# A macaron encoder layer on one core: seven-product blocks in the first up projection, and attention scores in three rounded passes

## The reference, cut to what matters

```
c_act = silu(c)
mod = (c_act @ w_ada + b_ada).reshape(B, 3, 3, D)        # shift, scale, gate of each sub-layer
h = x * (1 + scale) + shift
g, u = split(h @ ffn1_w_in, 2);  y = (silu(g) * u) @ ffn1_w_out            # 1024 -> 2 x 2816 -> 1024
x = layernorm(ALPHA * x + 0.5 * gate * y)
proj = h @ w_in;  cq, ckv, k_rope_raw, u = split(proj)
s = (q_nope . k_nope + q_rope . k_rope) * sm_scale       # 8 heads, 64 + 32 wide, chunk-causal
out = softmax(where(mask, s, -inf)) @ v
y = concat([out, pooled(u)]) @ w_out
... a second FFN like the first
```

## Time and profile before

| | |
|---|---|
| time, median of 3 runs (lowest, highest) | 938.01 us (937.66, 938.11) |
| the profiled execution's own time | 938.53 us |
| its span, from first to last instruction | 936.7 us |
| PE busy, share of the span | 924.4 us, 99% |
| DVE, ACT, POOL busy | 600.4, 422.3, 276.1 us |
| TensorE clock granted, mean | 0.998 |

### The profile page before, as it was taken

One profiled execution on the slowest core, in us unless ns is written; L12 is line 12 of the kernel. 1 busy time (PEld: TensorE's weight loads), 2 busy tenths in 40 slices (PEclk: granted clock), 3 DMA queues, 4 the chain that ended last, 5 costly groups with the idle time before them and its releaser, 6 DMA issues.

```text
span 936.7 us, 12697 instructions
## 1 busy us (share of the span) xinstructions
PE 924.4 (99%) x4845; PEld 777.8 (83%) x4845; DVE 600.4 (64%) x875; ACT 422.3 (45%) x673; POOL 276.1 (29%) x239
## 2 busy tenths in 40 slices
PE   8999999999999999999999999999999999999997
PEld 5788888888888888787776677889999999888886
DVE  6956776545454964687775577787777877533334
ACT  6753223332322132483576646655556555322124
POOL 0021111111113522155863655832111110035124
PEclk9999999999999999999999999999999999999999
DMA  9936556556553663314411112286777775623302
GB/s 356 379 117 211 189 192 199 193 180 206 192 175 129 200 240 116 102 68 135 118 63 46 45 54 82 70 255 158 183 190 180 179 193 147 225 79 107 124 18 90
DMA packets 50507, 144.88 MB, mean 155 GB/s; under 512 B 5264, under 2 KB 7440, under 8 KB 50448
## 3 DMA queue, kind: packets, MB, share of 16 engines
q1 hardware_dynamic: 45008, 134.65, 42.3%
q0 software_dynamic: 4896, 8.92, 6.0%
q10 hardware_dynamic: 544, 0.52, 0.2%
HBM read 138.83 MB, written 4.19 MB: 153 GB/s over the span
## 4 chain that ended last, share of the span: by engine, by line
PE 94%; DVE 2%; DMA 2%; ACT 1%; issue 1%; SPq 1%; ACTq 0%; DVEq 0%
PE bank L890 23%; PE bank L892 23%; PE bank L891 23%; PE bank L1001 6%; PE bank L1003 6%; PE bank L1002 6%; PE bank L1307 2%; PE bank L1331 1%; DMA ada_first<-ada_w 1%; PE bank L1318 1%; DMA raw_d<-wunits 1%; PE bank L975 1%; PE bank L1071 1%; PE bank L976 1%; PE bank L969 1%
## 5 line engine op out<-in xcount | busy, mean ns | idle before, releaser
L1434 DVE TENSOR_TENSOR w_lo<-raw,w_hi 128x1024 fp32r<-128x1024 f32 (+1 forms) x117 | 160.7, 1383 | 132.2 <-ACT w_hi L1406 131.8
L890 PE MATMUL bank<-h_hi,w_hi 128*128 128x512 f32 x455 | 178.7, 393 | 0.0
L892 PE MATMUL bank<-h_hi,w_lo 128*128 128x512 f32 x455 | 177.2, 389 | 0.0
L891 PE MATMUL bank<-h_lo,w_hi 128*128 128x512 f32 x455 | 177.2, 389 | 0.0
L1406 ACT ACTIVATE w_hi<-raw 128x1024 fp32r<-128x1024 f32 (+1 forms) x118 | 118.7, 1023 | 117.5 <-PE bank L892 111.5
L890 PE MATMUL bank<-a_hi,w_hi 128*128 128x512 f32 (+1 forms) x338 | 128.0, 379 | 0.0
L891 PE MATMUL bank<-a_lo,w_hi 128*128 128x512 f32 (+1 forms) x338 | 127.7, 378 | 0.0
L892 PE MATMUL bank<-a_hi,w_lo 128*128 128x512 f32 (+1 forms) x338 | 127.7, 378 | 0.0
L2542 POOL TENSOR_TENSOR a_lo<-act_t,a_hi 128x512 fp32r<-128x512 f32 x27 | 37.8, 1398 | 251.2 <-ACT a_hi L1529 251.1
L892 PEld LDWEIGHTS bank<-h_hi,w_lo 128*128 128x128 f32 x455 | 85.4, 188 | 18.1
L890 PEld LDWEIGHTS bank<-h_hi,w_hi 128*128 128x128 f32 x455 | 85.4, 188 | 17.9 <-issue 0.5
(11 more groups left out here) (374 smaller groups left out, 1948.6 us busy)
## 6 DMA issues: line engine op xcount, KB each, us to landing
raw<-wunits SPq DMA_DIRECT2D x110, 512.0 KB, 3.3
ada_ring<-ada_w SPq DMA_DIRECT2D x56, 512.0 KB, 4.3
raw_ab<-wunits SPq DMA_DIRECT2D x18, 512.0 KB, 4.7
ada_first<-ada_w SPq DMA_DIRECT2D x16, 512.0 KB, 11.1
raw<-wunits SPq DMA_DIRECT2D x32, 256.0 KB, 3.7
raw<-wunits POOLq DMA_DIRECT2D x32, 256.0 KB, 4.8
raw<-wunits SPq DMA_DIRECT2D x16, 384.0 KB, 2.9
raw_d<-wunits SPq DMA_DIRECT2D x17, 256.0 KB, 2.8
```

The costliest lines, as they stand in the source:

```text
L890: mm(out, lh, rh, start=first, stop=False)
L891: mm(out, lh, rl, start=False, stop=False)
L892: return mm(out, ll, rh, start=False, stop=last)
L1434: nc.vector.tensor_tensor(lo, raw_of(n, width), hi.bitcast(F32), SUB).then_inc(s_lo, 1)
```

## The change

Two things change. **First**, pairs 13 to 21 of the first up projection are done as blocks, with the code of the second FFN; pairs are numbered through (13 to 21, and 27 to 43 for the second FFN), and buffers for sums, copies and spilled x exist for both. Since the space of the modulation ring and DVE's time are taken there, the dots are spread anew: none in pairs 11 to 21, up to three per pair in pairs 3 to 10 (20 in all), and 36 in the down projection, one to three per unit, through a ring of four tiles. `c_act` is overwritten by block data and is loaded and activated again behind the blocks; x is read back there too. **Second**, the scores are three-pass products: ACT rounds K and Q (`k_high`, `q_high`), DVE (POOL for K of heads 4 to 7) writes the rests (`k_low`, `q_low`), and `scores` is `mm3`.

```diff
-ROPE_FIRST, ROPE_ACT = 4, 16
+ROPE_CHUNKS = {3: (0,), 4: (1,), 5: (2,), 6: (3,), 7: (4,), 8: (5,), 9: (6,), 10: (7, 8)}
+K_LOW_AFTER = {2: 4, 8: 5, 10: 6, 12: 7}
-T0 = 5
-D2 = F2 + 2 * T0
+FIRST, END = (13, FT + 5), (FT, 2 * FT)
+EDGE = (F1 + 2 * FIRST[0], F2 + 2 * (FIRST[1] - FT))
+D2 = EDGE[1]
+DOWN_AT = (F1_DOWN, D2)
+DOTS_UP = [0] * EARLY + [1, 1] * 2 + [1, 2] * 4 + [1, 1] * 2
+DOTS_DOWN = [0, 3, 3, 1, 1, 1] + [2, 3, 2] * 3 + [2, 2, 2]
+RING = 4
+ADA_UP = sum(DOTS_UP)
...
+        def ring_slot(a):
+            i = a % RING
+            if i < 2:
+                return ada_ring[:, i, :]
+            return ring_a[i - 2][:] if a < ADA_UP else (ring_norm, ring_act)[i - 2][:]
...
             def ada(a):
-                if a >= 2:
-                    sp.wait_ge(s_adadone, ADA_FIRST + a - 1)
-                sp.dma_start(ada_ring[:, a % 2, :], ada_w[ADA_FIRST + a]).then_inc(s_ada[a % 2], 16)
+                sp.wait_ge(s_adadone, ADA_FIRST + a - RING + 1)
+                sp.dma_start(ring_slot(a), ada_w[ADA_FIRST + a]).then_inc(s_ada[a % RING], 16)
...
+                if i == EARLY + 4:
+                    sp.wait_ge(*res_done(0))
+                    spill_x(0)
+            load_blocks(0)
+            sp.wait_ge(s_blk, PRODUCT["p3", END[0] - 1])
+            sp.dma_start(c_act[:], c_rows).then_inc(s_c, 16)
+            sp.wait_ge(s_bsum, SUM["gb", END[0] - 1])
+            ada(ADA_UP)
+            reload_x(0, 0)
+            ada(ADA_UP + 1)
+            reload_x(0, 1)
+            ada(ADA_UP + 2)
+            reload_x(0, 2)
+            reload_x(0, 3)
+            sp.wait_ge(s_al[0], FT)
+            ada(ADA_UP + 3)
+            unit(F1_DOWN + LEAD + 2)
+            for i, tiles in enumerate(ADA_STEPS):
+                unit(F1_DOWN + LEAD + 3 + i)
+                for a in tiles:
+                    if a + RING < RING_TILES:
+                        ada(a + RING)
...
-                    if p == 3 and m == 0 and j == 0:
-                        fourth_product(FT - 1)
-                        third_product(FT - 1)
+                    if p != 2 and m == 0 and j == 0:
+                        fourth_product(END[p // 2] - 1)
+                        third_product(END[p // 2] - 1)
...
-                    for t in range(EARLY // 2, FT):
+                    for t in range(EARLY // 2, FIRST[0]):
                         up(base, f, t)
...
-                    block_products()
+                block_products(f)
...
                 if i == 0:
-                    q_ready(pe, hd)
+                    pe.wait_ge(s_ql, QL_0 + hd + 1)
+                    pe.wait_ge(*((s_kl, KL_0 + hd + 1) if hd < K_DVE else (s_klp, KLP_0 + hd - K_DVE + 1)))
                 if k >= 2:
                     pe.wait_ge(s_exp, k - 1)
-                mm(bank[S_BANK[k % 2]][:, 0:(i + 1) * P], Q[:, hd % QRING, i * P:(i + 1) * P],
-                   K[:, hd, 0:(i + 1) * P], start=True, stop=True).then_inc(s_s, 1)
+                rows, keys = slice(i * P, (i + 1) * P), slice(0, (i + 1) * P)
+                mm3(bank[S_BANK[k % 2]][:, keys], (Q_hi[:, hd % QRING, rows], Q_lo[:, hd % QRING, rows]),
+                    (K_hi[:, hd, keys], K_lo[:, hd, keys]), True, True).then_inc(s_s, 1)
...
+                        if f == 0 and m == 0 and j == 1:
+                            act.wait_ge(s_c, 32)
+                            fn(c_act[:], c_act[:], ACT.Silu).then_inc(s_cact, 1)
...
+            def k_high(hd):
+                if hd == 0:
+                    act.wait_ge(s_kall, 32)
+                    act.wait_ge(s_mst, 2)
+                    act.wait_ge(s_full, KKV + KQ)
+                    emptied(act, T_V - 1)
+                fn(K_hi[:, hd, :], K[:, hd, :], ACT.Copy).then_inc(s_kh, 1)
+            def q_high(hd):
+                act.wait_ge(*((s_evd, sum(EVD[:T_Q + hd + 1])) if hd < 2 else (s_qr, hd - 1)))
+                act.wait_ge(*((s_eva, sum(EVA[:T_Q + hd + 1])) if hd < 2 else (s_qn, hd - 1)))
+                fn(Q_hi[:, hd % QRING, :], Q[:, hd % QRING, :], ACT.Copy).then_inc(s_qh, 1)
...
+                if step - 2 in FILL_STEP[1::2]:
+                    gi = FILL_STEP[1::2].index(step - 2)
+                    if FILL[gi][0] == "q":
+                        q_high(int(FILL[gi][1]))          # on DVE at the same steps: q_low
...
+            def q_low(hd):
+                dve.wait_ge(s_qh, QH_0 + hd + 1)
+                tt(Q_lo[:, hd % QRING, :], Q[:, hd % QRING, :], Q_hi[:, hd % QRING, :].bitcast(F32), SUB).then_inc(s_ql, 1)
...
+                if step in K_LOW_AFTER:                   # POOL
+                    hd = K_LOW_AFTER[step]
+                    pool.wait_ge(s_kh, KH_0 + hd + 1)
+                    tt(K_lo[:, hd, :], K[:, hd, :], K_hi[:, hd, :].bitcast(F32), SUB).then_inc(s_klp, 1)
```

813 lines of the change are left out of this document (475 added, 338 removed).

## The result

The change made the kernel slower, by 17.9 us on the medians where 5.0 were forecast.

What follows compares the result with a forecast made beforehand. PE, busy for 99% of the span, was taken to bound the kernel. The terms -7.2 + 1.0 + 4.4 + 4.2 + 4.0 - 1.4 = +5.0 us on the profiled 938.53 gave 943.5, 943.0 for the median; range 935 to 949.

Steps and rivals of the forecast that it cites:

- a: First up projection: nine pairs done as blocks save 0.80 us each on PE, -7.2 us.
- b: Edge of the new block stage: idle time at its start, DVE's three dots per pair held for hidden; +1.0 us.
- c: First down projection: late load of unit 5 and DVE's added dots make PE wait; +4.4 us (0.5 to 8).
- d: Front of the attention: ACT's roundings wait for K's rotary rows and delay the first exponential; +4.2 us (2 to 6).
- e: Softmax steps: rests of Q on DVE wait for ACT and delay mask, maximum and exponential; +4.0 us (1.5 to 6).
- f: Attention scores: three-pass products take PE less time than float32 ones; -1.4 us (-2.0 to +2.6).
- rival 5: PE idles about 2.8 us before scores of steps 0 and 2, the clock falls to 1.2 GHz; 946 us, chance 0.10.
- 1: The attention hides more: d and e cost 2 us instead of 8.2; 936.8 us, chance 0.14.
- 2: The first down projection is not late, so 4.4 us falls away; 938.6 us, chance 0.09.
- Rival 3: PE never waits, three units of lead absorb all lateness of DVE and ACT; -7.8 us, 930.2 us, chance 0.13.
- 4: Rounded score passes of 128 columns each cost a whole float32 product; f becomes +0.4, 945.3 us, chance 0.09.

Runs made afterwards that it cites:

- keep_warm: The changed kernel with 18 idle products on PE ahead of the scores of step 0 and 8 ahead of those of step 6; 953.59 us.
- blocks_only: The changed kernel with the attention of the kernel before: float32 scores, no roundings or rests of K and Q; 940.78 us, ratio 1.003.
- k_later: The changed kernel with seven of the eight roundings of K moved from the attention's front to behind later exponentials; 953.37 us.
- dots24: blocks_only with unit 5's load issued first, 24 dots in the up projection and at most 6 for each of tiles 1 to 6; 932.11 us, ratio 0.9939.
- dots_small: blocks_only with the 36 dots in the first down projection cut to 64 of 1024 elements, their waits and loads kept; 933.49 us.
- small_parts: The changed kernel with roundings and rests of K and Q cut to 32 of 512 columns, and float32 scores of plain Q and K; 947.14 us.

## Why the prediction was wrong, step by step

The direction was right. The size, +5.0, was not: +21.0 on the profiled execution, +17.9 on the medians. The median's loss splits by experiment into 2.6 for the block part and 14.9 for the attention part, where the forecast had -1.8 (a to c) and +6.8 (d to f). The block part was off by 4.4 us and of the wrong sign, the attention part by 8.1.

Three steps of the prediction failed, and in the profiled execution they hold about 13 of the 16.0 us between forecast and result: in c, that DVE behind tile 3 "loses no more", and what stood ahead of it (9.4 us for 4.4); in e and f, that the steps behind step 9 cost 0.4 us and gain 1.4 (3.6 us for -1.0); and in the sum, that the clock holds (about 3.3 us for 0). The edge of the blocks adds 1.4. With the clock held, as in keep_warm's trace, the attention up to step 9 came out close to the forecast: 4.8 us later than before at the scores of step 2 (forecast d, 4.2), and 3.9 more from there to step 9 (forecast 3.6).

**a and b, blocks and their edge: -6.2 forecast, -4.84 in the profile.** The pace was right: in the new stage block matmuls start 0.12 us apart (211.68, 211.80, 211.92 in PE's timeline). The edge cost 2.2 us, not 1.0, most of it in one place, where PE idles 1.6 us for DVE's `act_t`. That wait varies between the kernels' profiles (none in blocks_only, 0.6 us in k_later, 1.2 in dots24), which nothing here settles. In the pairs ahead of the blocks DVE's row adds up to 10.5 to 11.1 us by the prediction's own numbers, not 10 to 10.9; no wait came of it.

**c, the down projection: +4.4 forecast, +9.40 in the profile.** The late unit 5 and the late DVE were both there. The first cost 1.9 us, not 1.0. The second met its size, 2.7 for 2.6, partly by luck: between the residuals of tiles 0 and 1 the trace has five dots for three, not six for two, their cover was the idle time ahead of the `shift` copy and not the 2.66 us ahead of the residual, and the residual came 3.0 us late, not 1.9. With the 3.8 us of the next tile (forecast 3.9), the residual of tile 2 was 6.8 us late, not 5.8; the slack behind it was 1.9 us, not 1.4.

What failed most is the sentence "DVE stays behind but loses no more". I took a tile with seven dots for 14.8 us of DVE; from residual to residual it took 332.73 - 316.53 = 16.2 in blocks_only, PE's tile 14.96. I had left out the 1.4 us in which DVE waits for ACT behind each residual. (By the trace two tiles have seven dots, not three.) So the tiles behind tile 3 lost another 3.4 us in that trace. In the changed kernel's own trace these later waits are 2.2 (behind 1.9, 0.3 and 2.7 up to tile 3). The low clock behind the 2.7 takes up to 1.7 there, but only in place of waits: without it the stretch was as long (keep_warm). dots_small shows that all but about 2 us of the loss is DVE's time. The loads per tile are 5.1 MB, not 4.9, which changes nothing. POOL's part is as the earlier trace rows showed it: dots and rests beside it take 2.3 us for 1.2. The Trainium skill ("SBUF — State Buffer", the row on the shared port pair in its section of terms) says that DVE and GpSimd take turns at one pair of ports, the loser blocked for the whole instruction; the 1.1 us longer per dot or rest, and POOL's 2.27 us for 1.28, fit that.

**d, the front: +4.2 forecast, by the scores of step 2; +4.8 with the clock held, +7.4 in the profile.** The scores of step 0 came 4.57 us late, not 2.8; ahead of those of step 2 PE did not wait at all, since the low clock had made it late itself. The count of ACT's row was right in its parts, but it held only ACT. Between the rotary rows (469.46) and the Q copy (478.41) stand hops that I gave no price: the rest of a unit on DVE, behind ACT's rounding of that unit, which stood behind the last K; the scaled pool groups behind that rest; their rounding on ACT (1.58 us idle), and only then Q. By k_later, 3.4 of the 4.6 us are due to the place of the K roundings.

**e, the rests of Q: +4.0 forecast.** The waits at steps 6 and 9 came, 2.26 and 0.92 us, each behind DVE's wait for ACT, as forecast. The step that failed is "three more heads have products of other kinds between, and I take 0.4 for all of them". Behind step 9 PE waits 1.85 us for a copy of transposed probabilities ahead of the first product with V, 0.78 ahead of step 15, 0.83 for Q_lo of head 6 at step 24, and 1.03 more for a copy. ACT has 16 operations more, DVE 12 and POOL 4 (about 0.6 us each on ACT and 0.7 on DVE), in a stage in which these engines already set the pace at many steps. From step 9 on, where no fall of the clock mixes in, small_parts puts 1.2 us on the waits and the fixed time and 2.9 on the work as such. Chains were counted, and the load was not. For the whole attention the two can't be told apart so well: 6.4 us for the waits, 8.7 for the work with the falls of the clock that it brings.

**f, the scores: -1.4 forecast, 0.4 gained behind step 9, not to be told from 0 on the medians.** The paces were right but for the narrow scores:

```profile
549.70 0.33 PE L1047 MATMUL bank<-K_hi,lat 128*128 128x128 f32 x1
549.86 0.27 PE L1048 MATMUL bank<-K_lo,lat 128*128 128x128 f32 x1
549.98 0.28 PE L1049 MATMUL bank<-K_hi,Q_lo 128*128 128x128 f32 x1
550.09 0.41 PE L1478 MATMUL bank<-cols,cq 128*128 128x128 f32 x2
```

This is 0.39 us for 128 columns, where I had 0.34, and 0.69 for 512 (from 554.75 to 555.44). What failed is where it counts: behind step 9 PE waits at many steps too, so that most of the gain there is lost in waits.

**The clock, rival 5 (0.10): it happened, on top of the forecast.** I had it as a case apart, with 3 us. The size was right: the profiled execution lost about 3.3 us by it in the attention, and keep_warm gained 2.1 on the median by filling two of the gaps. But a forecast that itself has two gaps of 2.8 us on PE should not have kept the fall for a case of its own: gaps of 2.7 us in the down projection had it behind them in four profiles of nine, and those of 3.3 us and more ahead of step 0 in three of three. The Trainium skill ("TensorE: Matmul & The Clock Gate", section "Part 1: The HAM clock gate") calls the low clock the default, which activity releases. The windows agree: behind 4.4 us of idle time 0.50, and in 488 to 492, with PE busy throughout, 1.00.

Of the other rivals, 1, 2 and 3 are refuted by the traces (PE waits at every place named but step 2, and the times are far above theirs), and 4 by the distances above. Rival 3's sum does not follow from its terms either: with a, b, the low end of d (2) and half of f it is -4.9, 933.1 and not 930.2.

## What to carry to other kernels

Where the sum of added work is in a stage whose chains already run through three engines, count the load of each engine per step of the pipeline, not only the new waits: behind step 9 the work itself cost more than twice what its waits did. A small job (a dot, a rest) goes where a window of the trace shows its engine idle, and ahead of a maximum or residual nothing may stand that waits for another engine. And a gap of 2 to 3 us on PE is to be priced with the clock that may fall behind it, but only where PE then sets the pace: in the down projection, where DVE did, the fall cost nothing.
